# First layer's mixer: modulation chunks at other pieces, gated unit's evictions behind the attention steps of their slot

## What is computed

```python
m_lat = split((silu_c @ mod_w[layer] + mod_b[layer]), 6)      # the same for the context
h = rms_norm(x, norm1_g) * (1 + m[1]) + m[0]
z = h @ ev_w_in                                               # 1792 columns, latent and context
o = window_attention(rope(q), rope(k), v, ..., sink)          # 8 heads, 2 kv heads
u, v = split(gelu(z[..., 768:]), 2)                           # the gated unit
s = u * (w_s @ layer_norm(v) + b_s)
x = x + m[2] * (concat([o, s]) @ ev_w_out)
...
x = x + m[5] * expert_choice_ffn(h2, router_w, w1, w3, w2)
```

## Time and profile before

| | |
|---|---|
| median of three runs | 2285.45 us (2283.03 to 2288.56) |
| profiled execution | 2283.55 us, its span 2281.7 us |
| PE busy | 1986.4 us, 87% of the span |
| DVE, ACT busy | 999.4 us (44%), 749.9 us (33%) |
| DMA | 643.79 MB, mean 282 GB/s |
| the mixer of layer 0, 60 to 212 us | PE busy 142.78 of 152.00 us |
| experts of layer 0 and what follows, 352 to 930 us | PE busy 516.02 of 578.00 us, mostly waiting for chunks of the stream |

### The profile page before, as it was taken

How to read it: one execution, slowest core, us unless ns; L and a number is a source line. 1 busy time by engine, 2 the same in 40 slices (tenths; PEclk the granted TensorE clock), 3 DMA queues, 4 the chain that set the end, 5 groups by cost and what they waited for, 6 DMA issues and landing times.

```text
span 2281.7 us, 37943 instructions
## 1 busy us (share of the span) xinstructions
PE 1986.4 (87%) x16424; PEld 1479.2 (65%) x16424; DVE 999.4 (44%) x1906; ACT 749.9 (33%) x1336; POOL 11.7 (1%) x25
## 2 busy tenths in 40 slices
PE   6999899989897999756656658999999999999998
PEld 5777665444443767544444435878888878788887
DVE  3445522222121646311111104666677766556766
ACT  3344400000000645100000004665454456555444
POOL 0000000000000000000000000000000000000000
PEclk9999999999999999888788888999999999999999
DMA  9868379999999545599999996334555543355551
GB/s 392 341 227 346 131 330 427 427 427 427 427 428 427 199 148 221 236 427 426 426 427 426 427 426 253 143 138 174 195 185 185 191 178 131 129 189 205 196 195 56
DMA packets 46179, 643.79 MB, mean 282 GB/s; under 512 B 5264, under 2 KB 5536, under 8 KB 6592
## 3 DMA queue, kind: packets, MB, share of 16 engines
q1 hardware_dynamic: 43776, 628.75, 68.0%
q0 software_dynamic: 2240, 12.63, 1.4%
HBM read 640.31 MB, written 1.05 MB: 281 GB/s over the span
## 4 chain that ended last, share of the span: by engine, by line
PE 61%; DMA 31%; DVE 4%; ACT 3%; issue 1%; SPq 0%; DVEq 0%; ACTq 0%
PE bank L952 58%; DMA ring<-in_stream 30%; PE bank L960 3%; DMA x<-in_x_in 0%; ACT ring L1883 0%; ACT weights_high L1696 0%; DVE ring L2469 0%; DVE weights_low L2727 0%; DVE arena L2827 0%; ACT tokens_high_low L2047 0%; ACT arena L1718 0%; DVE arena L2343 0%; DVE arena L2178 0%; ACT arena L1729 0%; ACT arena L2013 0%
## 5 line engine op out<-in xcount | busy, mean ns | idle before, releaser
L952 PE MATMUL bank<-ring,arena 128*32 128x128 f32 (+5 forms) x7716 | 626.9, 380 | 211.0 <-DMA ring<-in_stream 207.5
L952 PEld LDWEIGHTS bank<-ring,arena 128*32 128x32 f32 (+2 forms) x7716 | 368.0, 135 | 439.4 <-DMA ring<-in_stream 263.6
L2727 DVE TENSOR_TENSOR weights_low<-ring,weights_high 128x1024 fp32r<-128x1024 f32 (+2 forms) x288 | 343.3, 1193 | 257.9 <-ACT weights_high L1696 256.9
L1696 ACT ACTIVATE weights_high<-ring 128x1024 fp32r<-128x1024 f32 (+2 forms) x288 | 297.7, 1035 | 278.1 <-PE bank L952 255.3
L952 PE MATMUL bank<-weights_high,tokens_high_low 128*128 128x512 f32 x960 | 313.7, 398 | 5.9 <-DVE tokens_high_low L2739 4.5
L2387 DVE TENSOR_TENSOR arena<-arena,bank 128x256 f32<-128x256 f32 (+1 forms) x64 | 22.7, 354 | 445.4 <-PE bank L952 445.4
L952 PEld LDWEIGHTS bank<-weights_high,tokens_high_low 128*128 128x128 f32 x960 | 180.9, 188 | 51.2 <-issue 7.1
L1844 ACT ACTIVATE arena<-bank 128x256 f32<-128x256 f32 (+1 forms) x64 | 21.1, 330 | 575.7 <-PE bank L952 575.7
L1696 ACT ACTIVATE arena<-bank 128x256 f32<-128x256 f32 (+6 forms) x218 | 84.4, 414 | 360.7 <-PE bank L960 302.7
L952 PE MATMUL bank<-weights_low,tokens_high_low 128*128 128x512 f32 x480 | 187.9, 392 | 0.0
L2397 DVE TENSOR_TENSOR arena<-bank,arena 32x512 f32<-32x512 f32 (+1 forms) x128 | 70.9, 554 | 255.8 <-PE bank L952 254.2
(11 more groups left out here) (252 smaller groups left out, 2192.6 us busy)
## 6 DMA issues: line engine op xcount, KB each, us to landing
ring<-in_stream SPq DMA_DIRECT2D x298, 2048.0 KB, 20.9
arena<-in_stream POOLq DMA_DIRECT2D x7, 1024.0 KB, 9.5
x<-in_x_in SPq DMA_DIRECT2D x1, 2048.0 KB, 10.9
arena<-in_od_pack POOLq DMA_DIRECT2D x1, 1024.0 KB, 5.0
x<-in_stream POOLq DMA_DIRECT2D x1, 1024.0 KB, 13.4
arena<-in_gains POOLq DMA_DIRECT2D x2, 512.0 KB, 5.8
out<-arena SPq DMA_DIRECT2D x1, 1024.0 KB, 4.0
arena<-in_b_masks POOLq DMA_DIRECT2D x1, 896.0 KB, 9.7
```

Of the source, the lines that this page charges most:

```text
L952: ins = pe.matmul(o, lhsT, rhs, start=start, stop=stop)
L1696: ins = act.activation(o, i, ACT.Copy)
L2727: dve.tensor_tensor(dst, whole, high.bitcast(F32), ALU.subtract).then_inc(sig, 1)
```

## The change

Three things. The modulation chunks of slots 11, 15, 19 go one slot later, and with them layer 1's: they now stand at 20 to 31 without a gap. `MODS_SAVED` goes from 16 to 17. For the chunks of the gated unit (1, complete at slot 23, and 0, complete at slot 31) ACT evicts behind the slot's attention steps and not ahead of them; and the next chunk's piece 0 (slots 24 and 32) stands on PE behind that slot's small steps and not ahead of them.

```diff
--- before.py
+++ after.py
@@ -96,9 +96,10 @@
 EV_TURNS = {11: (0, 1, 2), 19: (3, 4)}
 EV_ROPES = {8: (0, 128, 6), 16: (1, 512, 4)}
 MODS_FIRST, MODS_NEXT, COLUMNS_NEXT = (0, 2), {1: (0, 1), 2: (0, 3)}, 2
-EV_MODS = {**MODS_NEXT, **dict(zip((6, 7, 8, 9, 10, 11, 14, 15), ((0, c) for c in range(4, 12)))),
-           **dict(zip((19, 20, 21, 22, 23, 24, 25, 26, 27, 28, 30, 31), ((1, c) for c in range(12))))}
-MODS_SAVED = 16
+EV_MODS = {**MODS_NEXT, **dict(zip((6, 7, 8, 9, 10, 12, 14, 16), ((0, c) for c in range(4, 12)))),
+           **dict(zip(range(20, 32), ((1, c) for c in range(12))))}
+MODS_SAVED = 17
+GATED_UNIT = (0, 1)
 SGU_STATS, SGU_ROOT, SGU_V, SGU_AT = (24, 25), 26, 27, 31
 CAT_HEADS = {26: 0, 27: 1, 29: 2, 31: 3}
 CAT_TURNS = {34: (4, 5), 35: (6, 7)}
@@ -1319,8 +1320,12 @@
                         mm(bank("sgu", t)[:, g * P:(g + 1) * P], ev_sguw[:, g, :], ev_v[:, t, g * P:(g + 1) * P],
                            True, True, fills("sgu", t) if g == 3 else None)
 
+            def after_gated_unit(p):
+
+                return 0 < p <= EVZ_END and p % KD == 0 and EVZ_ORDER[p // KD - 1] in GATED_UNIT
+
             for p in range(A_END):
-                if not in_tail(*Z_PIECES[p]):
+                if not in_tail(*Z_PIECES[p]) and not after_gated_unit(p):
                     z_product(*Z_PIECES[p])
                 for j in EV_TURNS.get(p, ()):
                     ev_columns(j)
@@ -1339,6 +1344,8 @@
                     mod_cols(0, 1)
                 if unit_at(p, EV_S_AT) is not None:
                     ev_scores(unit_at(p, EV_S_AT))
+                if after_gated_unit(p):
+                    z_product(*Z_PIECES[p])
                 if p == SGU_AT:
                     sgu()
                     owed.extend(SPARE_SLOTS)
@@ -1884,8 +1891,9 @@
                                    accum_out=l[:, at:at + 1]).then_inc(sem("ev_p"), 1)
 
             def after_slot(p):
-                if p < EVZ_END and p % KD == KD - 1:
-                    ev_z_out(EVZ_ORDER[p // KD])
+                complete = EVZ_ORDER[p // KD] if p < EVZ_END and p % KD == KD - 1 else None
+                if complete is not None and complete not in GATED_UNIT:
+                    ev_z_out(complete)
                 for j in EV_TURNS.get(p, ()):
                     b.filled("evqk", j)
                     copy(ev_kt[:, :] if j == 0 else ev_qt[:, j - 1, :], bank("evqk", j)[:, :], frees("evqk", j))
@@ -1898,6 +1906,8 @@
                     copy(ev_ot[:, j, t * P:(t + 1) * P], bank("evatt", ("o", u))[:, 0:P], frees("evatt", ("o", u)))
                 if unit_at(p, EV_S_AT) is not None:
                     ev_exp(unit_at(p, EV_S_AT))
+                if complete is not None and complete in GATED_UNIT:
+                    ev_z_out(complete)
                 if p == SGU_ROOT:
                     act.wait_ge(sem("sgu_var"), 4)
                     root(root4, 1, sem("sgu_root"))
```

## The result

| | before | changed |
|---|---|---|
| median (lowest to highest), 14 runs each | 2284.30 us (2282.76 to 2289.71) | 2291.0 us (2284.86 to 2296.19) |
| ratio of the runs, 95% interval | | 1.0023 [1.0016, 1.0031] |
| profiled execution, span | 2283.55 us, 2281.7 us | 2292.88 us, 2290.6 us |
| first expert matmul of layer 0 (PE, tile `arena`) | 283.66 us | 294.38 us |

The changed kernel is slower by 0.23%, 5.3 us by the ratio (3.7 to 7.1; the two medians lie 6.7 us apart). The forecast of 2290.0 us (2284.0 to 2294.0) holds the measured 2291.0. What follows shows that it holds it partly for another reason than it gave.

The account below looks back on a forecast made before the run. The prediction took layer 0's mixer to be bound by PE and its waits. Its terms, 1.5 + 1.0 - 1.0 + 1.9 + 1.2 = +4.6 us, gave 2290.0 us on the median, range 2284.0 to 2294.0.

Parts of the forecast that it names:

- What bounds the kernel: Layer 0's mixer is bound by PE and its waits; what is lost before 212 us reaches the end one for one.
- Slots 23 and 24, +1.5: The 2.3 us wait ahead of scores 10 goes, 3.8 us of idle ahead of scores 11 comes: +1.5 us.
- The table load: ACT's GELU table load ahead of the evictions, priced at about 1.29 us from the trace; the skill's 2.66 would add 1.4.
- Slots 15 to 17, +1.0 at full clock: Scores start earlier in slot 15, piece 16 waits about 2.4 us for DVE's copy, slot 16 grows; together +1.0 us.
- Slot 19, -1.0: The modulation chunk leaves slot 19, but scores 6 then wait for ACT's first copy: -1.0 us.
- slot 29, +1.9: Slot 29 has no scores and no wait, so the modulation chunk put there costs its full time: +1.9 us.
- slot 27, 0: The modulation chunk comes earlier and the wait for ACT grows by as much: no change.
- The clock, 1.2 us in slot 24: The new 3.8 us idle stretch lowers PE's clock, costing nothing to 1.4 us, taken as 1.2; 2.2 us stretches do not.
- more falls: Rival: slot 16's stretch also lowers the clock or slot 28's chunk is late; +1.5 to +2 more, 2291.8 us, chance 0.10.
- The signs that I had named: Wrong if scores 11 start under 2 us after the chunk, slots 15-19 cost over 1 us, or experts' start ignores mixer's loss.
- the wait is really gone: Rival: ACT's evictions end before slot 24's modulation chunk, so scores 11 do not wait; sum -0.4, 2285.0 us, chance 0.12.

Follow-up runs that it names:

- after_again: The changed kernel profiled once more, for its clock; one run, no ratio: scores 9 to 12 took 26.92 us (26.93 in the changed kernel's first profile).
- evict_under_max: Kernel before, with ACT's evictions behind its copies but ahead of the exponentials and PE's piece between slot 24's modulation chunk and scores; ratio to before 0.9981 [0.9972, 0.9990].
- act_late_only: Kernel before with only ACT's evictions moved behind the exponentials, PE's piece unmoved; one run, no ratio: scores 9 to 12 took 30.20 us (before 24.04).
- mods_11_15: Kernel before with only layer 0's modulation chunks of slots 11 and 15 and the column turns one slot later; ratio to before 1.0013 [1.0003, 1.0023].
- before_again: The kernel before, unchanged, profiled once more for its clock; one run, no ratio: scores 9 to 12 took 25.59 us (24.04 in the first profile).
- warm_24: The changed kernel with slot 24's modulation chunk computed three times into the same bank, to keep PE at work; ratio to before 1.0029 [1.0019, 1.0040].

## Why the prediction was right, and where it was not

- *What bounds the kernel.* Right as far as shown: what the mixer lost arrived at the end, within the scatter of what follows it (1992.8 to 2000.5). That scatter is wider than the whole change, so "one for one" is not shown more closely.
- *Slots 23 and 24, +1.5.* Right in its parts: no wait ahead of scores 10, 8.31 us from scores 10 to 11 (8.3). The idle stretch read 3.3 and not 3.8, since the chunk waited 0.26 us for its data and slot 24's steps took 0.2 us longer than in the earlier trace rows.
- *The table load.* The 1.28 of the row held again, with the GELU 1.30 behind its start in the profile after. The figure of the Trainium skill ("ScalarE: Activation LUTs", What ACT_TABLE_LOAD costs), 2.66 us with a drain, would by an estimate have put scores 11 at 9.7. The trace shows no drain and decides against it.
- *Slots 15 to 17, +1.0 at full clock.* The waits came as said (2.49 us ahead of piece 16, 0.20 ahead of scores 4). after_again has 2.7 us more from scores 1 to 4, with one fall of about 1.5: order costs some 1.2.
- *Slot 19, -1.0; slot 29, +1.9; slot 27, 0.* Measured -1.04, +1.73 to +1.88, and 8.46 us from scores 13 to 14 before and after.
- *The clock, 1.2 us in slot 24.* This step failed: one error made the term too large, by about 0.6 us, and the other too small, by about 2.4. I read from one execution that stretches of 2.23 and 2.27 us do not lower the clock. They do, in most executions, so the kernel before pays too, and the new stretch adds about 0.6 us to that and not 1.2. And I kept the falls in slot 16 for a rival with a chance of 0.10; they came in five profiles of five, 1.5 us each, and in slot 20 in three of five, 0.9 on the mean, where I had none. In place of 1.2 stand about 0.6 + 1.5 + 0.9 = 3.0 us, and the sum is 3.4 + 3.0 = 6.4 us, against 5.3 (3.7 to 7.1) by the ratio. What happened was thus the case of "more falls", without its late transfer, to which I had given 0.10. That its price differs so little from the forecast's, and that the median came out at 2291.0 beside 2290.0, is luck as far as the clock goes.
- *The signs that I had named.* One of those for being wrong came true: slots 15 to 19 cost more than 1 us together. From the turns of slot 15 to piece 20 it is 30.16 us before and 31.94 in the profile after (+1.8), 31.85 in after_again; without the fall in piece 16 it would be 0.3, so it is the clock there and not the order. And the experts' first matmul was 10.7 and 2.7 us later in the two pairs, not 3 to 5: one execution of each kernel does not show this sign either way.
- *The rivals.* That the wait is really gone did not happen; its condition, an eviction block done before the modulation chunk ends, is what evict_under_max then made.

## What to carry to other kernels

When an eviction block is moved behind something, ask what stands behind it now: here it left the path of one unit's scores and came onto the path of the next, with the work that had covered it moved away too. The better place began in the time in which the engine waited anyway, between its copies and a maximum that another engine had yet to make; what did not fit delayed only work that was needed two slots later. And a stretch that did not lower the clock in one profile has not shown that it never will: two or three profiles of the kernel before are cheap, and give the price of the stretch that a change takes away as well as of the one it adds.

## What the runs showed of the hardware

- The clock fell behind idle stretches of 2.1 to 3.0 us in some executions and not in others of nearly the same instructions. Between 60 and 212 us a fall cost 1.3 to 1.6 us in most places, 2.2 behind 6.22 us of idle (act_late_only) and 2.7 behind 2.83 us (mods_11_15, at 76 us: a chunk of 3.57 and a piece of 2.58 us, in the other profiles 1.88 and 1.53). In the before_again profile the 2.27 us stretch of the earlier trace rows is followed by a granted clock of 0.89 over 150 to 165 us, where the first profile had 1.00 over the same bounds (and over those of the earlier trace rows):

```profile
150.00:165.00 15.00, 12.73 (x159) 10.18 (x161) 5.07 (x19) 10.37 (x23) 0.00 (x0) 0.89 0.73 274
```

- It also fell in slot 20 behind two short stretches, 0.65 and 0.79 us with one output between them, in three profiles of five, and in none of the eight others that have the chunk there. What sets it apart from the two that kept the clock these runs do not show.
- The two passes that warm_24 adds (128 matmul records on line 1052: x123 ahead of the gap, x3 and x2 behind it) met a gap of 1.74 us put down to issue, with nothing to wait for. It was seen once, and no run looked for its cause.
